# A mixture-of-experts stage on one Trainium2 core: expert passes of 32 slots on four column tiles instead of 64 slots on two

## What is computed

```python
def moe(h, w_router, b_router, w_gate, b_gate, w_up, b_up, w_down, b_down):   # h: 256 x 1024
    logits = jnp.dot(h, w_router) + b_router                # 32 experts
    top_logit, top_idx = lax.top_k(logits, 4)
    gates = jax.nn.softmax(top_logit, axis=-1)
...
        g = jnp.minimum(xb @ w_gate[e] + b_gate[e], 7.0)    # each w is 1024 x 1024 of one expert
        u = jnp.clip(xb @ w_up[e] + b_up[e], -7.0, 7.0)
        act = g * jax.nn.sigmoid(1.702 * g) * (u + 1)
        return act @ w_down[e] + b_down[e]
...
    y_pairs = ys[dest] * pair_gate[:, None]
    return jnp.zeros_like(h).at[pair_tok].add(y_pairs)
```

```
22 29 25 37 37  5 12 32   47 41 54 24 25 51 35 13
28 55 32 30 68 10 39 41   23 39 36 36 33 21 11 33
```

## Time and profile before

| | us |
|---|---|
| median of three runs | 1847.85 |
| the profiled execution | 1845.13 |
| its span (first to last instruction) | 1843.3 |
| TensorE busy in the span | 1799.4 (98%) |
| products with the experts' weights, L1402 and L1456, busy | 465.5 and 233.9 |
| VectorE busy, ScalarE busy | 605.5, 371.8 |
| bytes moved by DMA | 558.61 MB |

### The profile page before, as it was taken

The page is one execution under the profiler, slowest core; times in us unless marked ns, Lnnn a source line. Parts: engine busy times, 40 slices in busy tenths (PEclk is TensorE's granted clock), DMA queues, the critical chain, the costliest instruction groups (busy, mean ns, idle before and its releaser), DMA issues. The chain is left out here.

```text
span 1843.3 us, 23681 instructions
## 1 busy us (share of the span) xinstructions
PE 1799.4 (98%) x9487; PEld 1003.5 (54%) x9488; DVE 605.5 (33%) x1262; ACT 371.8 (20%) x721; POOL 10.9 (1%) x14
## 2 busy tenths in 40 slices
PE   7999899999999999999999999999999999999998
PEld 6757533333333333333333335767995466699843
DVE  1854411111111011011011013544655544345555
ACT  3222411111111111111111113332220033222101
POOL 0000000000000000000000000000000000000001
PEclk9999999999999999999999999999999999999999
DMA  9996699999999999999999999432446443124452
GB/s 379 390 191 271 261 418 430 431 431 431 432 432 431 432 431 431 432 431 432 431 431 431 432 431 329 156 142 92 151 149 241 160 182 137 46 92 149 149 176 98
DMA packets 104495, 558.61 MB, mean 303 GB/s; under 512 B 17128, under 2 KB 33997, under 8 KB 78701
## 3 DMA queue, kind: packets, MB, share of 16 engines
q1 hardware_dynamic: 101876, 553.06, 74.3%
q10 hardware_dynamic: 2554, 4.63, 1.8%
HBM read 552.43 MB, written 5.23 MB: 303 GB/s over the span
## 5 line engine op out<-in xcount | busy, mean ns | idle before, releaser
L1402 PE MATMUL ps<-ring,xs 128*64 128x512 f32 x2112 | 465.5, 592 | 4.9 <-DMA ring<-in_w_up 2.5
L1402 PEld LDWEIGHTS ps<-ring,xs 128*64 128x64 f32 x2112 | 151.3, 137 | 307.6 <-issue 298.2
L1456 PE MATMUL ps<-ring,actT 128*64 128x512 f32 x1056 | 233.9, 595 | 0.0
L2274 PE MATMUL ps<-ring 128*128 128x512 f32 x448 | 192.8, 592 | 0.0
L1529 DVE TENSOR_SCALAR hT<-ps 128x512 f32<-128x512 f32 x33 | 22.8, 692 | 446.0 <-PE ps L1402 446.0
L1456 PEld LDWEIGHTS ps<-ring,actT 128*64 128x64 f32 x1056 | 72.9, 137 | 158.7 <-issue 136.8
L2274 PEld LDWEIGHTS ps<-ring 128*128 128x128 f32 x448 | 84.9, 190 | 105.7 <-issue 105.7
L2010 PE MATMUL ps<-hT,ring 128*128 128x256 f32 x512 | 117.9, 383 | 4.3 <-ACT hT L1654 2.9
L1531 DVE TENSOR_SCALAR hT<-ps 128x512 f32<-128x512 f32 x33 | 22.9, 693 | 263.5 <-PE ps L1402 263.5
L2010 PEld LDWEIGHTS ps<-hT,ring 128*128 128x128 f32 x512 | 94.7, 190 | 23.2 <-issue 5.9
L2228 PE MATMUL ps<-hT,ring 128*128 128x128 f32 x768 | 93.4, 275 | 0.2 <-ACT hT L1654 0.2
(11 more groups left out here) (455 smaller groups left out, 1812.4 us busy)
## 6 DMA issues: line engine op xcount, KB each, us to landing
ring<-in_w_gate SPq DMA_DIRECT2D x64, 2048.0 KB, 26.2
ring<-in_w_down SPq DMA_DIRECT2D x64, 2048.0 KB, 26.1
ring<-in_w_up SPq DMA_DIRECT2D x64, 2048.0 KB, 24.6
ring<-in_mlp_w SPq DMA_DIRECT2D x16, 2048.0 KB, 8.4
ring<-in_mlp_w SPq DMA_DIRECT2D x32, 1024.0 KB, 5.4
ring<-in_w_mod SPq DMA_DIRECT2D x8, 2048.0 KB, 12.2
ring<-in_odd_w_in SPq DMA_DIRECT2D x6, 2048.0 KB, 10.1
ring<-in_w_mod SPq DMA_DIRECT2D x16, 512.0 KB, 10.9
```

The costliest lines, as they stand in the source:

```text
L1402: mm = pe.matmul(ps[SLOTS * half:SLOTS * (half + 1), bank, :], xs[:, c % 4, c // 4 * SLOTS:(c // 4 + 1) * SLOTS], weights(v, 8 * part + c) ...
L1456: mm = pe.matmul(ps[SLOTS * half:SLOTS * (half + 1), Y, :], actT[:, f % 4, f // 4 * SLOTS:(f // 4 + 1) * SLOTS], weights(v, 16 + f)[:, hal ...
L2274: return pe.matmul(product_bank(layer, n), token, weight, start=(c == 0), stop=(c == PAIRS - 1))
```

## The change

`SLOTS` becomes 32, and all experts but the last get passes of 32 slots on four column tiles: tile h has its slots on PSUM partitions 32h to 32h+31 and output columns 256h to 256h+255. The last expert (31) keeps passes of 64 slots on two tiles. A class `Tiling` holds what differs, `MOST` and `LAST` are its two cases, and each step of a pass takes one of them.

```diff
-SLOTS = 64
+SLOTS, LAST_SLOTS = 32, 64
...
+class Tiling:
+    def __init__(self, slots):
+        self.slots, self.tiles = slots, P // slots
+        self.wide = D // self.tiles
+        self.turns = self.wide // P
+    def rows(self, h):
+        return slice(self.slots * h, self.slots * (h + 1))
+    def cols(self, h):
+        return slice(self.wide * h, self.wide * (h + 1))
...
+    MOST, LAST = Tiling(SLOTS), Tiling(LAST_SLOTS)
...
-                    for half in range(2):
-                        mm = pe.matmul(ps[SLOTS * half:SLOTS * (half + 1), bank, :], xs[:, c % 4, c // 4 * SLOTS:(c // 4 + 1) * SLOTS],
-                                       weights(v, 8 * part + c)[:, half * 512:(half + 1) * 512], start=False, stop=(c == C - 1),
-                                       skip_group_check=True)
+                    at = c % T.turns * P + c // T.turns * T.slots
+                    for h in range(T.tiles):
+                        mm = pe.matmul(ps[T.rows(h), bank, 0:T.wide], xs[:, at:at + T.slots], weights(v, 8 * part + c)[:, T.cols(h)],
+                                       start=False, stop=(c == C - 1), skip_group_check=True)
...
-                for b in range(4):
-                    mm = pe.transpose(ps[:, TURN, b * P:(b + 1) * P], g[:, b:512:4], ident)
+                for a in range(4):
+                    for lane in range(2):
+                        mm = pe.matmul(ps[64 * lane:64 * (lane + 1), TURN, a * P:(a + 1) * P], g[:, a::4], ident, start=True, stop=True)
...
-            expert(1, EXPERTS // TURN_EXPERTS, last, n)
-            pe.wait_ge(y_sb, n + 1)
-            combine(True, total_ps)
+            gather(LAST)
+            combine(MOST, False)
+            pe.wait_ge(xrow_sb, last + 2)
+            turn_x(LAST)
+            biases(LAST)
+            with pe.Fori(last, n) as i:
+                last_pass(i, 1, TURNS)
```

More of the change, by code:

```diff
@@ L1293, in stage_experts, with activations @@
         m.sem(f"e_{n}") for n in ("sig_ok", "xrow_sb", "xs_sb", "selT_sb", "actT_sb", "y_sb", "bdown_in"))
+    def activations(T):
+        return (flat[:, T.wide * j:T.wide * (j + 1)] for j in range(3))
     def first_pass(eng, at, low=1):
@@ L1418, in _, with turn_sel @@
[L1418 to L1436 removed]
+            def turn_sel(bank, at):
@@ L1454, in one_pass @@
                         arrived(v, turn, 4 + f // 4)
[L1455 to L1458 removed]
+                    at = f % 4 * 2 * T.slots + f // 4 * T.slots
+                    for h in range(T.tiles):
+                        mm = pe.matmul(ps[T.rows(h), Y, 0:T.wide], actT[:, at:at + T.slots], weights(v, 16 + f)[:, T.cols(h)],
+                                       start=(f == 0), stop=(f == C - 1), skip_group_check=True)
                     if f == C - 1:
@@ L1491, in _, with gathered @@
-            ins.then_inc(y_sb, 1)
-            put.then_inc(selT_sb, 1)
-            n = passes(act)
-            with act.Fori(0, n) as i:
+            def gathered(T, n):
+                act.wait_ge(x_ps, n)
+                act.copy(xrow[:, 0:T.wide], ps[:, TURN, 0:T.wide]).then_inc(xrow_sb, 1)
+                act.wait_ge(xt_ps, n)
+                act.copy(xs[:, 0:T.wide], ps[:, TURN, 0:T.wide]).then_inc(xs_sb, 1)
+            for h in range(MOST.tiles):
+                act.dma_start(y[MOST.rows(h), 0:MOST.wide], t["b_down"][0][:, MOST.cols(h)]).then_inc(bdown_in, 16)
@@ L1500, in _ @@
-                act.copy(xs[:].rearrange("p b n -> p (b n)"), ps[:, TURN, :]).then_inc(xs_sb, 1)
+                gathered(MOST, i + 2)
+                act.wait_ge(selt_ps, i + 1)
+                act.wait_ge(comb_ps, i + 1)
+                act.copy(selT[:].rearrange("p i n -> p (i n)"), ps[:, Y, MOST.wide:MOST.wide + QT * P]).then_inc(selT_sb, 1)
+                act.wait_ge(actT_ps, i + 1)
+                for lane in range(2):
+                    rows = slice(64 * lane, 64 * (lane + 1))
+                    turned = ps[rows, TURN, :].rearrange("p (c q n) -> p c q n", q=2, n=SLOTS)[:, :, lane, :]
+                    ins = act.copy(actT[rows, 0:2 * P].rearrange("p (c n) -> p c n", n=SLOTS), turned)
@@ L1501, in _ @@
+                ins.then_inc(actT_sb, 1)
+                act.wait_ge(down_ps, i + 1)
+                act.copy(y[:, 0:MOST.wide], ps[:, Y, 0:MOST.wide]).then_inc(y_sb, 1)
+            gathered(LAST, last + 2)
+            with act.Fori(last, n) as i:
+                g, _, sig = activations(LAST)
+                act.wait_ge(g_ok, i + 1)
+                act.activation(sig, g, ACT.Sigmoid, scale=ALPHA).then_inc(sig_ok, 1)
+                gathered(LAST, i + 3)
                 act.wait_ge(selt_ps, i + 1)
```

266 lines of the change are left out of this document (150 added, 116 removed).

## The result

| | before | after |
|---|---|---|
| median of 9 runs each, us | 1848.52 | 1853.15 |
| range, us | 1846.38 to 1852.35 | 1851.71 to 1856.65 |
| profiled execution: span, us | 1843.3 | 1850.5 |

The ratio is 1.0022, with an interval of 1.0012 to 1.0032. The forecast was 1838.5 us with a range of 1833 to 1845.

What follows compares the result with a forecast made beforehand. The experts' stage was near both TensorE's and the DMA's limits, with 14.8 us behind its last weights. Terms -3.7 - 1.3 + 2.8 - 8.3 + 0 + 1.2 = -9.3 us gave 1835.8 profiled, 1838.5 as median; range 1833 to 1845.

Steps and rivals of the forecast that it cites:

- 4: Rival: the weights' stream ends the stage and small things eat the rest; gain under 3.7 us, 1846; chance 0.05.
- The new pass: One pass of an expert on four tiles takes 15.5 us, range 14.5 to 17.5, instead of 27.3.
- rival 1: The new pass takes over 16.2 us, TensorE late at the stage's end; at 17.2 us, 1847; chance 0.12.
- 3: Rival: four tiles don't run side by side, so there are 16 more passes of 27 us; 2285; chance 0.02.
- Rival 2: TensorE's clock stays low in the bursts and returns only in the wide last pass; slower, 1859; chance 0.05.
- (a): Start of the experts' stage: TensorE's first expand begins earlier and its first half is shorter; -3.7 us (-1.6 to -4.6).
- (b): First gaps in the weights' stream, 233.1 to 290.0 us, where DMA moved 421 GB/s, not 431: -1.3 us, up to -2.5.
- (c): Expert 20's three passes hold its six places until the third, so expert 21's fifth part comes late; +2.8 us (0 to +6).
- The stream: First new weights to the last: one part in 4.87 us except near expert 20; +1.5 us with (b) and (c).
- (d): End of the experts' stage: last combine 6.5 us behind the last weights where it was 14.8; -8.3 us.
- (e): Next stage: its loads keep up, between nothing and 1.3 us late; taken as 0.
- (f): TensorE's clock falls at times while waiting for weights, costing in (c) and the hand-over of (d); +1.2 us in all.

Runs made afterwards that it cites:

- a_nine: The changed kernel with a ring of nine places and a loop of three experts per turn instead of ten and five; 1850.83 us, ratio 1.0011.
- a_nine_cap: The changed kernel with nine places, turns of three experts and at most two passes per expert (expert 20's last 4 tokens left out); 1843.66 us, ratio 0.9978.
- b_nine: The kernel before the change with nine places and three experts per turn; 1852.18 us, ratio 1.0022.
- a_unroll: The changed kernel with TensorE's turn loop written out as six turns without a jump back between them; 1849.32 us, ratio 1.0005.
- a_nine_cap_tiny: a_nine_cap with 25 tiny matmuls ahead of each expert of TensorE's turn loop; 1898.73 us, ratio 1.0272.
- b_split: The kernel before the change with every 512-column product with expert weights cut into two of 256 columns; 1889.68 us, ratio 1.022.
- b_down: The kernel before the change with only the products with w_down cut in pieces of 256 columns; 1887.52 us, ratio 1.0216.
- a_cap: The changed kernel with at most two passes per expert, leaving out expert 20's last 4 tokens; 1849.63 us, ratio 1.0006.
- a_nine_pad: a_nine with 100 already fulfilled waits ahead of each expert of TensorE's turn loop; 2011.3 us in its only run.
- a_warm: The changed kernel with four more clock-keeping matmuls in the routing; 1853.84 us, ratio 1.0027.

## Why the prediction was wrong

What decided was in none of my terms and none of my rivals: the size of TensorE's code. My description of the change counted what each record costs in time and never what it takes as an instruction. The rival nearest to it, 4, had the right place (the stream ends the stage) and no mechanism.

- **The new pass, 15.5 us:** right, 15.54. So is what was built on it: TensorE idles in front of the weights (62.6 us in all; I had written some 120, of which standstills took a part), and rivals 1 and 3 fell. Rival 2 didn't come either, though TensorE's clock fell 18 times in the stage, where it didn't fall once in the kernel before. Three slips in the working change nothing in the forecast: counted from 1, slice 6 of the earlier trace rows has 418 GB/s and the unbroken stretch is 7 to 24; the list of passes in rival 1 adds up to ten, and nine are those behind expert 25's first; and "the rest divided" leaves rival 1 a chance of 0.03 to be faster, not 0.06.
- **(a) Start, -3.7:** measured -0.4. The first `gather` began 1.6 us later, not 0; the chain from there to `expand` was 5.36 instead of 7.07 us, 1.7 of the 2.1 that I had counted. The other half of the term was half an `expand` in 1.8 us; with the clock at 0.5 it took 224.94 - 221.30 = 3.64. With nine places it came: first new weights at 233.7 in `a_nine`, 234.1 in `a_nine_cap` and 237.9 in `b_nine`. In `a_nine` the clock was up in the first `expand` (3.66 us); in `a_nine_cap` it wasn't (5.03), but the first `gather` began 1.7 us earlier than in `b_nine`, so its -3.8 is in part luck. What delays the changed kernel's start stays open.
- **(b) First gaps, -1.3:** not earned: up to 510 us the stream fell 3.6 behind where before had 1.7. Without fetches it is 0.1 in `a_nine_cap` and 1.0 in `a_nine`.
- **(c) Three passes, +2.8:** right, 2.2. The fifth part of expert 21 was issued at 820.20, 19.3 us behind expert 20's last landing (forecast 19.2), and landed after 7.6 us (7.9). The table has 4.0 for this stretch, but the two landings behind it came on time (4.84 and 4.86 us); the rest is 1.0 at the part that landed at 843.3, after 16.9 us in the queue and with a code fetch at 839, and smaller amounts elsewhere. The same sum for nine places gives 27.1 - 4 x 4.87 = 7.6; `a_nine` had 7.3.
- **The stream, +1.5 with (b) and (c):** measured +12.9. **This is the step that failed.** The prediction let the DMA bring one part in 4.87 us from end to end but for expert 20, and had no term for code that travels on the same engines. Of the 11.4 us between, 1.3 are a term (b) that was not earned, 2.1 are the hole at 510 to 560, and 8.6 are spread over the whole stream; expert 20 came 0.6 under its term. In `a_unroll` the hole is 1.3 smaller. That the rest is the fetches' doing is shown by the table, where it is in all three kernels that fetch and in none of the three that don't, and by `a_nine_cap_tiny`, which differs from `a_nine_cap` in nothing but 300 instructions per turn.
- **(d) End, -8.3:** measured -5.5, a second and smaller miss. Expert 30 ended at 1099.53 + 1.93 = 1101.5, 27.2 us before the last weights (27.3). The next rows show the rest:

```profile
1099.53 1.93 PE L1443 MATMUL ps<-ring,actT 128*32 128x256 f32 x32 [1.76 <-DMA ring<-in_w_down]
1102.15 1.94 PE L1386 MATMUL ps<-x_sb,sel 128*64 128x512 f32 x8 [0.69 <-ACT y L1565]
1104.02 1.15 PE L1433 MATMUL ps<-selT,y 32*128 32x256 f32 x16
1105.09 0.75 PE L1392 MATMUL ps<-consts_sb,xrow 128*128 128x128 f32 x4
1105.77 1.09 PE L1399 MATMUL ps<-brows,now 32*64 32x512 f32 x8
1106.79 7.09 PE L1418 MATMUL ps<-ring,xs 128*64 128x512 f32 x32
...
1125.57 1.68 PE L1399 MATMUL ps<-brows,now 32*64 32x512 f32 x8
1127.17 8.15 PE L1443 MATMUL ps<-ring,actT 128*64 128x512 f32 x32
1136.01 2.00 PE L1433 MATMUL ps<-selT,y 64*128 64x256 f32 x16 [0.69 <-ACT y L1579]
```

  The hand-over is 1106.79 - 1101.46 = 5.3 us instead of 4.1: `biases` (1.1 us) was missing from my list, and `gather` stands behind the wait for `y` (0.7). The clock fell in the last `biases` and product, 0.6 and 1.1 us; that was (f).
- **(e) Next stage, 0:** right; the last `combine` ended 7.1 us later than before and the span grew by 7.2.
- **(f) Clock, +1.2:** 1.7 in the last pass, and 1.8 in the first `expand`, a place that I had not named.

That the plan itself was sound shows where both causes are out: `a_nine_cap` against `b_nine` is 1843.66 to 1852.18 us, -8.5; the profiled spans, 1843.1 and 1852.4, are 9.3 apart: a start of -3.8, a stream of 0 and an end of -5.5. The four tokens that it leaves out cost `a_nine` 7.2 us of it. No kernel that computes everything was found to beat the one before; `a_unroll` is level with it.

## What to carry to other kernels

Twice the column tiles nearly halved the time of a pass (27.3 to 15.5 us) and nearly doubled its instructions (297 to 540): before a loop body is widened or unrolled, count its instructions in the compiled program and compare the page's packets of the instruction queue with what they were. Where a stage is bound by its DMA, a loop body that no longer stays in the engine can cost twice: by standstills at the jumps back, which weigh where the engine has no time to spare (30 us in `b_split` and `b_down`, whose times rose by 40), and by a stream that falls behind by about 1% throughout, which was most of the loss here. A stream's lateness, tabled by stretch and against one part's time, tells such causes apart sooner than the total does.

## What the runs showed of the hardware

- TensorE kept a loop body of 1620 instructions (101 KiB) without fetching it again (49 packets), and not one of 1770 (111 KiB, 130 packets). The Trainium skill, "Runtime: NRT & Kernel Launch", section Instruction fetch mechanics, gives TensorE 2048 instructions, in blocks of 256, and says that a taken branch out of the window stops the engine for a fetch. The runs agree on blocks (packets of 16 KiB, 256 instructions of 64 bytes) and stop; the measured limit for a loop lies lower than 2048, between 1620 and 1770. By the Trainium skill the window is two blocks, which these runs don't bear out: loops of 1485 and 1620 instructions jumped back without a fetch.
- A jump back to code that isn't kept stopped TensorE for 6.9 to 7.1 us in the changed kernel, 5.7 to 6.2 in `b_split` and `b_down` and up to 8.2 in `a_cap`. Behind it the granted clock is 0.50 (780.6 to 784.0 in the changed kernel), and an `expand` of 7.04 us took 8.67 in `b_down` (659.09). Straight on, no stop was over 0.6 us (`a_unroll`).
- Fetches of code slow down other transfers: with 26 packets of 16 KiB from 560 to 800 us the weights of `a_nine_cap_tiny` fell 3.8 us behind one part in 4.87, with 20 those of the changed kernel 2.4, and with none those of `a_nine_cap` gained 0.4.
- An instruction of TensorE that only waits, for something that has come long since, took 0.10 to 0.12 us (`a_nine_pad`).
- Between the turn loop's entry and the first `expand` "issue" was 1.9 to 2.1 us in the changed kernel and `a_warm`, 1.5 in the kernel before and in `b_split`, 1.2 in `b_nine`, 0.8 and 1.1 in `a_nine_cap` and `a_nine`, and 0.6 with no loop. The size of the body isn't what sets it, since `b_split` has 2445 instructions and the kernel before 1485; what does wasn't tried.
